# Delta rule of a hybrid decoder step: inverse levels that update the transposed inverse, and couplings as products of 128 columns with the quadrants in turn

## The reference, cut to what matters

```python
incl = ii[:, None] >= ii[None, :]
...                                          # kb = kc * beta, vb = vc * beta, decay = exp(gcum_i - gcum_j)
eye_plus = I + strictly_lower((kb @ kc.T) * decay)
u = triangular_solve(eye_plus, vb, lower, unit_diagonal)
w = triangular_solve(eye_plus, kb * exp(gcum), lower, unit_diagonal)
qk = where(incl, (qc @ kc.T) * decay, 0)
def step(S, xs):                             # over the chunks, one after the other
    v_new = u_i - w_i @ S
    o = qg_i @ S + qk_i @ v_new
    S = S * gl_i + kg_i.T @ v_new
```

## Time and profile before

| what | us |
|---|---|
| median of 3 runs | 1061.8 (1059.75 to 1063.49) |
| profiled execution: span, first to last instruction | 1063.1 |
| profiled execution: time around the span | not listed apart from the span |
| TensorE matmul busy | 962.0 (90%) |
| VectorE busy | 452.7 (43%) |
| delta stage, from its first product to the last output DMA | 376.6 to 514.4 |
| rounds 0 to 11 in it | 392.8 to 483.2 |

### The profile page before, as it was taken

The page is one execution under the profiler, slowest core; times in us unless marked ns, Lnnn a source line. Parts: engine busy times, 40 slices in busy tenths (PEclk is TensorE's granted clock), DMA queues, the critical chain, the costliest instruction groups (busy, mean ns, idle before and its releaser), DMA issues. The chain is left out here.

```text
span 1063.1 us, 21210 instructions
## 1 busy us (share of the span) xinstructions
PE 962.0 (90%) x8122; PEld 635.4 (60%) x8122; DVE 452.7 (43%) x942; ACT 310.9 (29%) x714; POOL 266.5 (25%) x395
## 2 busy tenths in 40 slices
PE   6899999999899989998799998996599999998686
PEld 5456777777666858898455664454455555555342
DVE  2240000002767257786568772337532333333226
ACT  4100000000575213233467642101023232333232
POOL 6000000032102146900256523000222343444110
PEclk9899999999999989999699998997599998999898
DMA  9975642523920046000744252936699999999972
GB/s 312 348 276 216 211 177 100 115 81 80 308 83 7 1 82 148 4 4 8 188 116 124 73 180 109 298 133 245 237 334 378 387 395 378 385 372 367 372 261 94
DMA packets 90507, 212.18 MB, mean 200 GB/s; under 512 B 31730, under 2 KB 54954, under 8 KB 76510
## 3 DMA queue, kind: packets, MB, share of 16 engines
q1 hardware_dynamic: 77666, 187.36, 51.8%
q0 software_dynamic: 9984, 20.15, 6.0%
q10 hardware_dynamic: 2756, 3.27, 0.9%
HBM read 254.83 MB, written 33.95 MB: 272 GB/s over the span
## 5 line engine op out<-in xcount | busy, mean ns | idle before, releaser
L2801 DVE COPY mixT<-PS 128x128 f32<-128x128 f32 x49 | 14.3, 292 | 164.0 <-PE PS L2515 164.0
L592 PE MATMUL PS<-hT,wring 128*128 128x288 f32 x256 | 83.5, 408 | 0.0
L593 PE MATMUL PS<-hT,wring 128*128 128x288 f32 x256 | 83.0, 406 | 0.0
L2405 POOL DMA_INDIRECT ys_dram<-late,ids x47 | 43.4, 924 | 149.1 <-ACT late L2615 122.6
L2399 POOL DMA_INDIRECT mixT<-h_dram,ids x49 | 46.8, 956 | 111.4 <-DVE ids L2768 92.4
L2496 PE MATMUL PS<-ring,mixT 128*64 128x256 f32 x304 | 72.6, 394 | 1.6 <-DVE mixT L2787 1.5
L2497 PE MATMUL PS<-ring,mixT 128*64 128x256 f32 x304 | 72.6, 394 | 0.0
L2496 PEld LDWEIGHTS PS<-ring,mixT 128*64 128x64 f32 x304 | 43.1, 143 | 32.6 <-issue 12.1
L2429 PE MATMUL PS<-late,mixT 128*128 128x512 f32 x128 | 58.4, 617 | 1.8 <-PEq L2883 1.8
L592 PEld LDWEIGHTS PS<-hT,wring 128*128 128x128 f32 x256 | 48.2, 190 | 17.2 <-DVE xc L203 2.6
L593 PEld LDWEIGHTS PS<-hT,wring 128*128 128x128 f32 x256 | 48.6, 190 | 13.4
(11 more groups left out here) (575 smaller groups left out, 2212.5 us busy)
## 6 DMA issues: line engine op xcount, KB each, us to landing
ring<-in_expert_w_gate_dram SPq DMA_DIRECT2D x27, 1024.0 KB
ring<-in_expert_w_up_dram SPq DMA_DIRECT2D x27, 1024.0 KB
ring<-in_expert_w_down_dram SPq DMA_DIRECT2D x27, 1024.0 KB
late<-in_w_ada_dram SPq DMA_DIRECT2D x8, 2048.0 KB
mod_r<-in_expert_w_gate_dram SPq DMA_DIRECT2D x9, 1024.0 KB
mod_r<-in_expert_w_up_dram SPq DMA_DIRECT2D x9, 1024.0 KB
mod_r<-in_expert_w_down_dram SPq DMA_DIRECT2D x9, 1024.0 KB
late<-in_expert_w_gate_dram SPq DMA_DIRECT2D x7, 1024.0 KB
```

The costliest lines, as they stand in the source:

```text
L592: MM(PS[:, b, 0:HALF], lhs, hT[:, k, 0:HALF], **s)
L593: last = MM(PS[:, b + 1, 0:HALF], lhs, hT[:, k, HALF:NTOK], **s)
L2405: pool.indirect_dma_start(m.ys_dram.ap(), bass.IndirectOffsetOnAxis(ap=ids[:, 1, j:j + 1], axis=0), yr(n), None, bounds_check=LAST_ROW, oo ...
```

## The change

`level_p` takes its 16 products with the four quadrants in turn (`q`, then `h`, then `c`) and counts both halves at the end of its products. In all levels but a tile's last, `level_t` waits for both masks and computes the product the other way round, `Y` as weights and `Pm` as moving data, so that it gives the transposed update: row half `c`, column half `h`, bank by `c`, four quadrants in turn. `step` then subtracts it from `T`, not from `Y`; `turn` transposes `T`, and ScalarE copies the result into `Y`. In the last level `Y` is updated as before. `prep_c` makes one product per block with 128 moving columns, queries and keys side by side, 16 matmuls and not 32, in the order `mm`, `e`, `c`; the two results change places in their bank, and `couplings` reads them there. Waits are on the same semaphores and counts as before, except that `level_t` waits for both masks.

```diff
--- before.py
+++ after.py
@@ -1102,7 +1102,7 @@
         Y = m.raw[:, 0, 0:4 * W].rearrange("p (s n) -> p s n", s=4)
         Pm, U = [m.raw[:, 0, x * 2 * W:(x + 1) * 2 * W].rearrange("p (s n) -> p s n", s=2) for x in (2, 3)]
         bt = m.raw[:, 1, 0:4 * W].rearrange("p (s n) -> p s n", s=4)
-        btq, Yq, Pmq = [a.rearrange("p s (q h n) -> p s q h n", h=2, n=C) for a in (bt, Y, Pm)]
+        btq, Yq, Pmq, Tq = [a.rearrange("p s (q h n) -> p s q h n", h=2, n=C) for a in (bt, Y, Pm, T[:, :, :])]
         Ss = m.raw[:, 1, 4 * W:8 * W].rearrange("p (b m v) -> p b m v", b=NB, v=HD)
         kg = tb("kg", [P, TILES, W])
         wT = tb("wT", [P, 2, 2, M4, C])
@@ -1239,7 +1239,8 @@
             def turned(i, l):
                 for e in range(2):
                     act.wait_ge(tt_ps, tn(i, l, e))
-                    nc.scalar.copy(T[:, i % 2, e * HW:(e + 1) * HW], PS[:, bank(i, e), 0:HW]).then_inc(tt_ok, 1)
+                    to = Y[:, i % 4, :] if l else T[:, i % 2, :]
+                    nc.scalar.copy(to[:, e * HW:(e + 1) * HW], PS[:, bank(i, e), 0:HW]).then_inc(tt_ok, 1)
 
             def take_out(n):
                 i, c = n // 2, n % 2
@@ -1342,8 +1343,8 @@
                 two = lambda a: a.rearrange("p (e n) -> p e n", e=2)
                 dve.wait_ge(c_ps, i + 1)
                 dve.wait_ge(b1_ok, i + 1)
-                V.tensor_tensor(two(bt[:, i % 4, :]), PS[:, x:x + 2, 0:HW], two(bt[:, i % 4, :]), ALU.mult).then_inc(bt_ok, 1)
-                V.tensor_tensor(two(qk[:, i, :]), PS[:, x:x + 2, HW:W], two(dm[:, i % 2, :]), ALU.mult).then_inc(qk_ok, 1)
+                V.tensor_tensor(two(bt[:, i % 4, :]), PS[:, x:x + 2, HW:W], two(bt[:, i % 4, :]), ALU.mult).then_inc(bt_ok, 1)
+                V.tensor_tensor(two(qk[:, i, :]), PS[:, x:x + 2, 0:HW], two(dm[:, i % 2, :]), ALU.mult).then_inc(qk_ok, 1)
 
             def norm(i, part):
                 if part == 0:
@@ -1372,7 +1373,7 @@
 
             def step(i, l):
                 for h in range(2):
-                    y = Yq[:, i % 4, :, h, :]
+                    y = Yq[:, i % 4, :, h, :] if l == LAST[i] else Tq[:, i % 2, :, h, :]
                     dve.wait_ge(lt_ps, lv(i, l, h))
                     V.tensor_tensor(y, y, PS[:, bank(i, h), 0:HW].rearrange("p (q n) -> p q n", n=C), ALU.subtract).then_inc(lt_ok, 1)
 
@@ -1518,11 +1519,13 @@
                     pe.wait_ge(egb_ok, i + 1)
                     pe.wait_ge(b1_ok, i + 1)
                 x = BANKS[i][3]
-                for e, mm, c in blocks:
-                    tok = slice(i * P + c * C, i * P + (c + 1) * C)
-                    kT, q = m.yT[half[e], M4 + mm, tok], m.yT[half[e], mm, tok]
-                    MM(PS[half[c], x + e, mm * C:(mm + 1) * C], kT, kT, start=True, stop=True)
-                    last = MM(PS[half[c], x + e, HW + mm * C:HW + (mm + 1) * C], kT, q, start=True, stop=True)
+                for mm in range(M4):
+                    for e in range(2):
+                        for c in range(2):
+                            tok = slice(i * P + c * C, i * P + (c + 1) * C)
+                            q_and_k = m.yT[half[e], 0:2 * M4, tok].rearrange("p (s m) n -> p s m n", s=2)[:, :, mm, :]
+                            last = MM(PS[half[c], x + e, :].rearrange("p (s n) -> p s n", s=2)[:, :, mm * C:(mm + 1) * C],
+                                      m.yT[half[e], M4 + mm, tok], q_and_k, start=True, stop=True)
                 last.then_inc(c_ps, 1)
 
             def turn_out(i):
@@ -1548,27 +1551,39 @@
             def turn(i, l):
                 if l:
                     pe.wait_ge(lt_ok, lv(i, l, 1))
+                    src = T[:, i % 2, :]
                 else:
                     pe.wait_ge(y0_ok, i + 1)
                     if i >= 2:
                         pe.wait_ge(lt_ok, lv(i - 2, LAST[i - 2], 1))
+                    src = Y[:, i % 4, :]
                 for e in range(2):
                     for x in range(2):
-                        last = nc.tensor.transpose(PS[:, bank(i, e), col(x)], Y[:, i % 4, e * HW + x * P:e * HW + (x + 1) * P], m.ident[:, :])
+                        last = nc.tensor.transpose(PS[:, bank(i, e), col(x)], src[:, e * HW + x * P:e * HW + (x + 1) * P], m.ident[:, :])
                     last.then_inc(tt_ps, 1)
 
             def level_p(i, l):
                 pe.wait_ge(tt_ok, tn(i, l - 1, 1))
                 if l == 1:
                     pe.wait_ge(bw_ok, i + 1)
-                for h in range(2):
-                    for q in range(M4):
+                for q in range(M4):
+                    for h in range(2):
                         for c in range(2):
                             at = slice(q * P + c * C, q * P + (c + 1) * C)
                             last = MM(PS[half[c], bank(i, h), q * C:(q + 1) * C], bt[half[h], i % 4, at], T[half[h], i % 2, at], start=True, stop=True)
-                    last.then_inc(lp_ps, 1)
+                        if q == M4 - 1:
+                            last.then_inc(lp_ps, 1)
 
             def level_t(i, l):
+                if l < LAST[i]:
+                    pe.wait_ge(lp_ok, lv(i, l, 1))
+                    for q in range(M4):
+                        for h in range(2):
+                            for c in range(2):
+                                last = MM(PS[half[h], bank(i, c), q * C:(q + 1) * C], Yq[half[c], i % 4, q, h, :], Pmq[half[c], i % 2, q, h, :], start=True, stop=True)
+                                if q == M4 - 1 and h == 1:
+                                    last.then_inc(lt_ps, 1)
+                    return
                 for h in range(2):
                     pe.wait_ge(lp_ok, lv(i, l, h))
                     for q in range(M4):
```

## The result

The changed kernel takes 1054.6 us (median of 20 executions, 1048.6 to 1061.0) against 1062.7 (20 executions) for the kernel before: ratio 0.993 [0.991, 0.994], faster by 0.7%. Two of the 20 executions of before, 1403.7 and 2503.8, lie far from all others and don't count in the ratio. The profiled execution of the changed kernel has a span of 1056.0 us where that of before has 1063.1.

A forecast was written before the change was run, and what follows sets the result against it. TensorE was taken to be in flight almost without a break in rounds 0 to 5, both TensorE and VectorE full in rounds 6 to 8. Terms sum to 6.9 us off the median: 1054.9, said as 1055.0, range 1051.5 to 1061.5.

The forecast's parts named there:

- What a product costs: TensorE's small products: four quadrants in turn make `level_t` 0.93 us for two tiles, `level_p` 0.95 to 1.0, `prep_c` 0.90.
- Start: Start of the delta stage: `couplings` of tile 0 loses its wait for `prep_c`, -0.55 us.
- Round 0: Round 0, priced at half clock: `level_p` -0.7 and `level_t` -0.6, together -1.3 us.
- Round 1: Round 1: `prep_c` ends 0.95 us earlier and everything behind it on VectorE with it, -1.0 us.
- Round 2: Round 2: `level_p` some 0.4 us, `level_t` from 1.86 to 0.93, together -1.35 us.
- Round 3: Round 3: the same as round 1 again, -0.95 us.
- Round 5: Round 5: couplings' wait for `prep_c` gives -0.95 us, the steps' waits for `level_t` -0.2, together -1.15.
- Rounds 6 to 11: Rounds 6 to 11: VectorE busy without a gap, each round gives 0 to 0.1 us, -0.2 in all.
- VectorE takes it all: Rival, rounds 0 to 5: only the waits for `prep_c` go (3.4 us), even rounds give nothing; 1058.4 us, chance 0.14.
- Dear starts: Rival, TensorE: a start costs about 25 ns whatever the quadrant, the sum is zero; 1061.8 us, chance 0.05.
- quadrants in turn no faster: Rival, `level_p` and `prep_c`: quadrants in turn run no faster than two, so slower; 1067.8 us, chance 0.06.
- The clock falls in the new gaps: Rival, rounds 1 and 3: TensorE's idle under couplings brings two clock falls of 2.4 us; 1059.8 us, chance 0.12.

The follow-up runs named there:

- the other chip: Changed kernel, unchanged, timed on one chip beside 23 executions of the kernel before: 1055.9 us against 1058.6, ratio 0.997 [0.994, 1.000].
- the first pair: First traces of the kernel before and the changed kernel: spans 1063.1 and 1056.0 us, delta stage's stretch 113.1 and 105.3.
- the levels alone: Changed kernel with the old `prep_c` and `couplings`; 1057.0 us in a single execution.
- 64 columns: Changed kernel with `prep_c` as 64 passes of 64 columns, quadrants still in turn; 1061.9 us in a single execution.
- zero rows later: Changed kernel with the 18 DMAs that write zero rows waiting for the first state; 1053.9 us in a single execution.
- both edits: Changed kernel with `from_state` of rounds 6 to 8 ahead of the second turn and zero-row DMAs behind the fifth state; 1054.8 us, ratio 0.995 against before.
- state first: Changed kernel with `from_state` of rounds 6, 7, 8 moved between the turns of the two tiles; 1059.3 us in a single execution.

## Why the prediction was right

The forecast was 1055.0 with a span of 1056.2; measured 1054.6 and 1056.0. That is closer than its terms deserve, and in part luck: the forecast took 6.9 off a median of 1061.8, and the medians of the full comparison lie 8.1 apart, those of the other chip 2.7. What repeats is the 6.0 of the stretch. So term by term:

- *What a product costs*: right. 0.93 for `level_t` of two tiles, measured 0.94; `prep_c` 0.90 from 1.85, measured 0.82 from 1.79; `level_p` 0.95 to 1.0, measured 1.03 in rounds 1 and 3, 0.94 in rounds 6 to 8, and 1.35 (from 1.76) in rounds 2 and 4, where its first passes run among those of the swap (L1548). The rule of the Trainium skill that I weighed ("TensorE: Matmul & The Clock Gate", section "Wait — 56ns, not 53.3ns?") would have 64 passes take 1.6 us, an estimate from its 25 ns; 0.94 us is one start in 15 ns, so across quadrants the trace doesn't agree.
- *Start* −0.55: −0.63 in the first pair. Its own scatter (15.2 to 16.0 in the changed kernel) is as large as the term, so it is only not contradicted. The wait itself is gone.
- *Round 0* −1.3: −1.38 between the two traces with 6.8 us of low clock (9.92 and 8.54), −1.20 without any (the levels alone, 6.33 against 7.53). The −2.66 between the first traces is half low clock that was shorter, 3.4 us, and no gain.
- *Round 1* −1.0: −0.99 (6.48 to 5.49). The first trace of before held 0.34 more. *Round 2* −1.35: −1.19 to −1.32, 0.4 by `level_p` and the rest by `level_t`. *Round 4* −0.4: −0.41, all of it `level_p`.
- *Round 3* −0.95: −0.64 in the first pair, with −0.99 where no standstill falls in it (6.48 to 5.49). I took round 3 to be round 1 again; that holds for the waits, but not for the supply of instructions.
- *Round 5* −1.15: −0.87. The step that failed is "the steps behind lose their waits for `level_t`". They did not: before the last steps the wait grew from 0.31 to 0.54 while the two operations shrank from 0.89 to 0.75, so from the end of `new_state` to the end of these steps it is 1.29 us and was 1.20. These steps wait for a product that stands behind `products`, `from_state` and `to_state`, none of which became faster.
- *Rounds 6 to 11* −0.2: under 0.1 by the rounds, and the old levels there cost nothing.
- *Behind the stage*: I let the saving reach the end whole. In the first pair the stage gave 7.8, the part behind it took back 2.9, and the part ahead of it happened to be 2.2 shorter. Here the forecast had no term; scatter cancelled.

The rivals: *VectorE takes it all* is refuted by the even rounds, which give 1.2 to 1.3, 1.3 and 0.4; VectorE does set the pace in rounds 6 to 9, which gave nothing. *Dear starts* and *quadrants in turn no faster* fall with the 0.94. *The clock falls in the new gaps* did not happen where I placed it, between 400 and 483, in any trace of the changed kernel. It did in three of the experiments, each time behind a standstill: 3.4 us of low clock began 0.3 us after one of 1.94 (levels alone) and 1.5 us after ones of 2.37 (64 columns) and 1.45 (zero rows later), though not after the 1.70 of two others. And behind the stage, where I did not look, something of the kind may be at work.

## What to carry to other kernels

Of small products on 64x64 quadrants the order counted more than the width here: the 64 passes of `prep_c` took 1.79 us with two quadrants at a time and 1.04 to 1.09 with four in turn, and a width of 128 brought only the rest, to 0.82. If a product uses only two quadrants whatever its order, as the old `level_t` did, see whether its transpose uses four: 1.86 became 1.34 by that, and 0.94 with the order. Price such an edit by the round, asking which wait ends last there: `prep_c` paid in the odd rounds, the levels mostly in the even ones. Before you call two parts more than their sum, look in the traces of each for what neither edit made: here a standstill and a low clock took 0.7 us from the experiment with the levels alone. And where a stage repeats to hundredths inside an execution of 1055 us that scatters by 10, measure the stage, and set the clock of an execution beside its time.

## What I had not expected of the hardware

**TensorE stood still for want of instructions.** That it is instructions is read from the "issue", from the kind of the queue and from the timing; no view names the cause outright. Inside a group of passes with nothing to wait for, TensorE stood still for 0.3 to 2.4 us. In all 14 traces each such standstill in the rounds ended 2.25 to 2.8 us after the start of a 16 KB packet of the instruction queue q8. In the changed kernel that packet comes at 410.61, and the passes go on at 412.88. A stretch of 0.15 us around it:

```profile
DMA packets 12, 0.05 MB, mean 355 GB/s; under 512 B 2, under 2 KB 2, under 8 KB 11
## 3 DMA queue, kind: packets, MB, share of 16 engines
q1 hardware_dynamic: 11, 0.04, 116.2%
q8 instruction: 1, 0.02, 39.0%
```

q1 carries the zero rows. In the run with both edits the same packet, the nineteenth of q8, has the queues to itself (0.15 us from 409.80 on), and the `level_t` behind it runs through:

```profile
DMA packets 1, 0.02 MB, mean 109 GB/s; under 512 B 0, under 2 KB 0, under 8 KB 0
q8 instruction: 1, 0.02, 38.8%
...
413.11 1.11 PE L1584 MATMUL PS<-late 64*64 64x64 f32 x64
```

From start to start the standstills were 0.26 to 1.08 us in the kernel before (rounds 1 and 3) and 1.15 to 1.42 in the changed one (round 3), where VectorE's couplings cover most of it: the round is only 0.35 to 0.63 longer than 5.49; denser passes use up instructions faster, which fits but was not tested by itself. That the zero rows' traffic brings the standstills is shown by their move with it (rounds 3 to 7 and 8) and their absence without it. Only the two short ones at the beginning of round 4 (0.30 with the levels alone, 0.42 with 64 columns) lie in the first few us behind the traffic, under a low clock. What comes late is the packet's start: beside the zero rows the nineteenth packet starts 0.7 to 0.9 us before `level_t` of round 3 (the three traces of the changed kernel and state first), without them 2.9 (zero rows later, at 407.41) and 3.3 (both, at 409.80). Once started, the packets in and around the rounds take 0.9 to 1.5 us with the traffic and without. How the start is held up, and how early the packet is asked for, the traces don't show.
